# One encoder block on one core: router ahead of the norm, the prompt's sort in pairs of tiles, the two lists and first gathers apart

## The reference, cut to what matters

```python
x = x + concat(yA, yB) @ w_out                      # D = 1024; yA, yB are two attentions
h = rms_norm(x, ffn_norm_w)
aff = softmax(h @ w_router)                          # n tokens x 16 experts
gates, idx = top_k(aff.T, cap)                       # cap = 2 * n / 16: 128 prompt, 32 sample tokens
def expert(idx_e, g_e, wg, wu, wd):                  # D_EXPERT = 2816
    xe = h[idx_e]
    return ((silu(xe @ wg) * (xe @ wu)) @ wd) * g_e
x = x.at[idx].add(experts)
return rms_norm(x, final_norm_w)
```

## Time and profile before

| | us |
|---|---|
| median of 3 runs | 2697.51 (2696.32 to 2697.77) |
| span of the profiled execution, first to last instruction | 2693.8 |
| PE busy | 2606.6 (97%) |
| DVE busy | 1963.9 (73%) |
| ACT busy | 1692.7 (63%) |
| POOL busy | 1108.9 (41%) |

### The profile page before, as it was taken

How to read it: one execution, slowest core, us unless ns; L and a number is a source line. 1 busy time by engine, 2 the same in 40 slices (tenths; PEclk the granted TensorE clock), 3 DMA queues, 4 the chain that set the end, 5 groups by cost and what they waited for, 6 DMA issues and landing times. The chain is left out here.

```text
span 2693.8 us, 53857 instructions
## 1 busy us (share of the span) xinstructions
PE 2606.6 (97%) x22588; PEld 2372.4 (88%) x22588; DVE 1963.9 (73%) x2361; ACT 1692.7 (63%) x2527; POOL 1108.9 (41%) x781
## 2 busy tenths in 40 slices
PE   7999999989959999999999999999999999999997
PEld 6666776665549999999999999999999999999997
DVE  6233256674668788888878888787878878788787
ACT  4366345562127676676767677676766767677675
POOL 2224201134125364452736346263644627354354
PEclk9999999999969999999999999999999999999998
DMA  7311312124557898979889897988988798898887
GB/s 188 76 46 32 74 37 44 36 85 150 168 199 274 314 313 297 330 256 342 293 319 315 292 333 258 340 294 314 322 293 322 269 330 304 311 323 289 317 299 285
DMA packets 365898, 652.18 MB, mean 242 GB/s; under 512 B 26599, under 2 KB 94055, under 8 KB 365623
## 3 DMA queue, kind: packets, MB, share of 16 engines
q1 hardware_dynamic: 349483, 605.63, 64.5%
q0 software_dynamic: 16176, 43.12, 6.3%
HBM read 612.81 MB, written 36.94 MB: 241 GB/s over the span
## 5 line engine op out<-in xcount | busy, mean ns | idle before, releaser
L1986 DVE TENSOR_TENSOR wl<-stg,wh 128x2048 bf16<-128x2048 f32 (+1 forms) x544 | 1241.0, 2289 | 256.6 <-ACT wh L1476 251.8
L1476 ACT ACTIVATE wh<-stg 128x2048 fp32r<-128x2048 f32 (+1 forms) x544 | 1010.9, 1861 | 196.2 <-PE S L1104 71.4
L2379 POOL TENSOR_TENSOR hx<-hh,hx 128x320 fp32r<-128x320 f32 x176 | 385.6, 2191 | 805.9 <-ACT hx L1529 805.6
L1101 PE MATMUL S<-X,wh 128*128 128x320 f32 x3760 | 591.0, 312 | 1.3 <-DVE X L1995 1.3
L1101 PEld LDWEIGHTS S<-X,wh 128*128 128x128 f32 x3760 | 557.1, 189 | 1.7 <-DVE X L1995 1.7
L1147 PE MATMUL S<-hx,wh 128*128 128x320 f32 x1892 | 312.6, 313 | 0.5 <-DVE yTs L2034 0.5
L1101 PE MATMUL OG<-X,wh 128*128 128x320 f32 x1872 | 298.2, 311 | 1.2 <-DVE gg L2016 1.2
L1104 PE MATMUL S<-Xb,wl 128*128 128x160 bf16 x3760 | 290.1, 233 | 0.0
L1147 PEld LDWEIGHTS S<-hx,wh 128*128 128x128 f32 x1892 | 280.8, 188 | 0.9 <-issue 0.6
L1101 PEld LDWEIGHTS OG<-X,wh 128*128 128x128 f32 x1872 | 277.4, 188 | 1.6 <-issue 1.4
L1104 PEld LDWEIGHTS S<-Xb,wl 128*128 128x128 bf16 x3760 | 258.9, 98 | 12.0
(11 more groups left out here) (316 smaller groups left out, 3803.5 us busy)
## 6 DMA issues: line engine op xcount, KB each, us to landing
stg<-in_w_gate_dram SPq DMA_DIRECT2D x80, 2048.0 KB
stg<-in_w_up_dram SPq DMA_DIRECT2D x80, 2048.0 KB
stg<-in_w_down_dram SPq DMA_DIRECT2D x64, 2048.0 KB
stg<-in_w_down_dram SPq DMA_DIRECT2D x32, 1536.0 KB
stg<-in_w_gate_dram SPq DMA_DIRECT2D x16, 1024.0 KB
stg<-in_w_up_dram SPq DMA_DIRECT2D x16, 1024.0 KB
w_st<-in_w_in_dram SPq DMA_DIRECT2D x20, 512.0 KB, 4.0
yt<-mixed SPq DMA_DIRECT2D x10, 512.0 KB, 5.4
```

The costliest lines, as they stand in the source:

```text
L1101: pe.matmul(out, w, x, start=first, stop=False, skip_group_check=True)
L1476: act.activation(piece_conv(wh, g), piece_stage(g), ACT.Copy).then_inc(rounded, 1)
L1986: dve.tensor_tensor(piece_conv(wl, g), piece_stage(g), piece_conv(wh, g).bitcast(F32), ALU.subtract).then_inc(split, 1)
L2379: pool.tensor_tensor(hx[:, f, CT:2 * CT], hh[:, :, :], hx[:, f, 0:CT].bitcast(F32), ALU.subtract).then_inc(hidden_ready, 1)
```

## The change

- **The router goes ahead of the norm.** PE turns `x2t` instead of `h2t`; ACT (not DVE) copies the turned rows to `h2T`. The router matrix is multiplied once by the norm's weight (`fw_cols`, a new load of 1024 single elements; `wrt_scaled`), and each row's 1/rms is applied to the logits (`logits`: one fused multiply and maximum, then a subtraction).
- **Order of a turn.** Turn t now turns tile t-1's sum after two of the eight cross pairs of the first half, and turns its affinities before the last two cross pairs of the second half. Before, the affinities of tile t-2 were turned.
- **The last tile's sum is made in two halves**, as soon as each half is projected.
- **The sort is in pairs of tiles.** `WK` is 112 partitions of 64 values: both tiles of a pair, each in two halves. Eight rounds (the last without a replacement) rank them, `bitonic` steps merge halves, the pair, and the pair with the best so far. `SORTS` spreads these 31 units over turns 2 to 9 and the end. The sample has its own buffer `WS` and its own four rounds at the end.
- **Lists apart.** Cutoff, comparison, ranks and places of the prompt are made before those of the sample; prompt and sample row numbers of the first expert have a matmul and a semaphore step each. POOL gathers 128 prompt rows, then 32 whole sample rows (`xes`, by `idx_first`), in place of the two gathers of quarters. PE turns the prompt rows without waiting for the sample's. Later experts gather as before.

The diff, cut to its core:

```diff
-ROUNDS_AHEAD = {6: (0, 5, 6), 7: (0, 11, 12), 10: (1, 5, 6)}
-ROUNDS_BEHIND = {5: (0, 0, 5), 6: (0, 6, 11), 7: (0, 12, 16), 9: (1, 0, 5), 10: (1, 6, 11), 11: (1, 11, 12)}
+HALF_ROUNDS = 8
+U_PAIR = HALF_ROUNDS + 7
+U_BOTH = U_PAIR + 8
+U_ALL = U_BOTH + 8
+SORT_X2, SORT_H2, SORT_END = range(3)
+SORTS = {(2 * p + 2 + n, at_): (p, u0, u1) for p in range(TPR // 2) for n, at_, u0, u1 in
+         ((0, SORT_END, 0, 2), (1, SORT_X2, 2, 6), (1, SORT_H2, 6, 14), (1, SORT_END, 14, 15),
+          (2, SORT_X2, 15, 21), (2, SORT_H2, 21, U_ALL if p else U_BOTH)) if 2 * p + 2 + n < TT}
...
+                sp.dma_start(fw_cols[:, :], ffn_norm_w[0].rearrange("(k p) -> p k", p=P)).then_inc(wrt_in, 16)
...
-            for t in range(TT + 2):
-                if t < TT:
-                    wo_half(t, 0)
...
-                    pe.wait_ge(h2_ready, t)
-                    for c in range(2):
-                        turn(wo_fill["h", t - 1] + c, [h2t[:, b * P:(b + 1) * P] for b in range(4 * c, 4 * c + 4)])
+            pe.wait_ge(scores_read, 2 * STEPS)
+            for t in range(TT):
                 if t >= 2:
-                    aff_turn(t - 2)
-                if t < TT:
-                    wo_half(t, 1)
-                if 1 <= t <= TT:
-                    router(t - 1)
...
+                    wo_highs(t, 0, range(KT))
+                    wo_crosses(t, 0, (0, 1))
+                    x2_turn(t - 1, 0)
+                    x2_turn(t - 1, 1)
+                    mm = wo_crosses(t, 0, range(2, KT))
+                    if t == TT - 1:
+                        mm.then_inc(mixed_ready, 1)
+                    if t == 1:
+                        pe.wait_ge(wrt_scaled, 1)
+                        pe.wait_ge(out_read, STEPS)
+                    router_parts(t - 1, range(KT))
+                wo_highs(t, 1, range(KT))
+                if t + 1 < TT:
+                    y_turn(t + 1)
+                if t:
+                    router_sum(t - 1)
+                wo_crosses(t, 1, range(KT - 2))
+                if t:
+                    aff_turn(t - 1)
+                wo_crosses(t, 1, (KT - 2, KT - 1)).then_inc(mixed_ready, 1)
+
+            u = TT - 1
+            for c in range(2):
+                x2_turn(u, c)
+                router_parts(u, range(4 * c, 4 * c + 4))
+            router_sum(u)
...
+            index_p(1).then_inc(idx_ps, 1)
+            pe.wait_ge(onehot_ready, 2)
+            index_s(1, bank=1).then_inc(idx_ps, 1)
             pe.wait_ge(gathered, 16)
-            pe.wait_ge(gathered_s, 32)
+            pe.wait_ge(idx_ready, 3)
             for q in range(4):
-                x_turn(q, q)
+                for m in range(2):
+                    d = 2 * q + m
+                    mm = pe.transpose(x_banks[q][:, m * CP:(m + 1) * CP], xe[:, d * P:(d + 1) * P], identf[:, :])
+                mm.then_inc(xturned, 1)
+            pe.wait_ge(gathered_s, 16)
+            for d in range(KT):
+                mm = pe.transpose(S[:, 1, CS * d:CS * d + CS], xes[:, d * P:(d + 1) * P], identf[0:CS, 0:CS])
+            mm.then_inc(xturned, 1)
...
+                    if u < HALF_ROUNDS:
+                        if u == 0:
+                            dve.wait_ge(affT_ready, 2 * p + 2)
+                        eight = ranked[:, 8 * u:8 * u + 8]
+                        own(dve.max(eight, WK[:, :]))
+                        own.wait()
+                        if u < HALF_ROUNDS - 1:
+                            own(dve.match_replace(WK[:, :], eight, WK[:, :], -1.0))
+                            own.wait()
+                    elif u == HALF_ROUNDS:
+                        own(dve.tensor_copy(other[:, 0:64], ranked[64:112, ::-1]))
+                        own.wait()
+                        dve.tensor_tensor(m[0][:, 0:64], ranked[0:48, :], other[:, 0:64], ALU.max)
+                        own(dve.tensor_tensor(m[0][:, 64:128], ranked[0:48, :], other[:, 0:64], ALU.min))
+                        own.wait()
+                    elif u < U_PAIR:
+                        n = u - HALF_ROUNDS
+                        bitonic(m[(n - 1) % 2], m[n % 2], 64 >> n)
...
+                dve.wait_ge(mixed_ready, t)
+                x2_free(u)
+                x2_sum(u, slice(0, D))
+                dve.sem_inc(mixed_read, 1)
+                dve.sem_inc(x2_ready, 1)
+                if (t, SORT_X2) in SORTS:
+                    sort_units(*SORTS[t, SORT_X2])
+                h2_rows(u)
+                if (t, SORT_H2) in SORTS:
+                    sort_units(*SORTS[t, SORT_H2])
+                logits(u)
                 if t + 1 < TT:
                     y_lows(t + 1)
-                if t in ROUNDS_BEHIND:
-                    best_eight(part, 48, min(r0 + 2, r1), r1)
-                if t == 8:
-                    merge(0)
-                if t >= TT:
-                    affT_copy(t - 2)
-
-            dve.wait_ge(affT_ready, TT)
-            best_eight(1, 80, 12, 16)
-            dve.tensor_copy(least[32:48, :], ranked[64:80, 1, P - 1:P].to_broadcast([NE, P]))
-            merge(1)
-            own(dve.tensor_tensor(top2[:, :], merges[:, 2, :], merges[:, 3, ::-1], ALU.max))
+                affinities(u)
+                affT_copy(u)
+                if (t, SORT_END) in SORTS:
+                    sort_units(*SORTS[t, SORT_END])
...
+            x2_sum(u, slice(0, 512))
+            dve.sem_inc(x2_ready, 1)
+            dve.wait_ge(mixed_ready, TT + 1)
+            x2_sum(u, slice(512, D))
+            dve.sem_inc(x2_ready, 1)
+            sort_units(TPR // 2 - 1, U_PAIR, U_BOTH)
+            own(dve.tensor_tensor(best[1][:, :], best[0][:, :], merges[0][0:NE, ::-1], ALU.max))
             own.wait()
-            own(dve.tensor_reduce(cutoff[:, :], top2[:, :], AX_X, ALU.min))
+            own(dve.tensor_reduce(cutoff[:, :], best[1][:, :], AX_X, ALU.min))
             own.wait()
-            dve.tensor_copy(least[0:NE, :], cutoff[:, 0:1].to_broadcast([NE, P])).then_inc(cutoff_ready, 1)
-            dve.wait_ge(cutoff_ps, 1)
-            for t0, t1, e0 in ((0, TPR, 0), (TPR, TT, 32)):
-                lim = S[:, 0, e0:e0 + NE].unsqueeze(1).to_broadcast([P, t1 - t0, NE])
+            dve.tensor_copy(least[0][:, :], cutoff[:, 0:1].to_broadcast([NE, P])).then_inc(cutoff_ready, 1)
+            logits(u)
+            h2_rows(u)
...
+            affinities(u)
+            dve.wait_ge(cutoff_ps, 1)
+            dve.wait_ge(aff_ready, TT)
+            choose(0, TPR, S[:, 0, 256:256 + NE])
+            affT_copy(u)
+            dve.wait_ge(affT_ready, TT)
+            for r in range(CS // 8):
+                eight = ranked_s[:, 8 * r:8 * r + 8]
+                own(dve.max(eight, WS[:, :]))
+                own.wait()
+                if r < CS // 8 - 1:
+                    own(dve.match_replace(WS[:, :], eight, WS[:, :], -1.0))
+                    own.wait()
+            dve.tensor_copy(least[1][:, :], ranked_s[:, CS - 1:CS].to_broadcast([NE, P])).then_inc(cutoff_ready, 1)
...
+            list_places(0, TPR, S[:, 0, 0:2 * TPR * NE].rearrange("p (m t e) -> p m t e", m=2, t=TPR))
+            dve.wait_ge(cutoff_ps, 2)
+            choose(TPR, TT, S[:, 0, 768:768 + NE])
...
+            onehots_p(1).then_inc(onehot_ready, 1)
+            dve.wait_ge(pos_ps, 2)
+            dve.wait_ge(chosen_ready, 2)
+            list_places(TPR, TT, S[:, 0, 512:576].rearrange("p (m t e) -> p m t e", m=2, t=TT - TPR))
+            onehots_s(1).then_inc(onehot_ready, 1)
...
+            pool.wait_ge(h2_stored, 16 * TPR)
+            pool.wait_ge(idx_ready, 1)
+            stand()
+            pool.indirect_dma_start(xe[:, :], None, hn_d,
+                                    bass.IndirectOffsetOnAxis(ap=idx[:, 0, 0:1], axis=0)).then_inc(gathered, 16)
+            pool.wait_ge(h2_stored, 16 * TT)
+            pool.wait_ge(idx_ready, 2)
+            stand()
+            pool.indirect_dma_start(xes[:, :], None, hn_d,
+                                    bass.IndirectOffsetOnAxis(ap=idx_first[:, 0:1], axis=0)).then_inc(gathered_s, 16)
```

494 lines of the change are left out of this document (283 added, 211 removed).

## The result

| | before | after |
|---|---|---|
| median of the runs, us | 2697.51 | 2673.87 (2670.68 to 2675.89, 5 runs) |
| ratio, 95% interval | 1 | 0.9919 (0.9908 to 0.9929) |
| span of the profiled execution | 2693.8 | 2670.6 |
| its own time beside the span | not given | 2672.59 |
| start of the projection to PE's last cross (E) | 135.30 | 133.22 |

The account below looks back on a forecast made before the run. PE's own work bounds the expert stage; before it PE waits in a 42.3 us stretch, mostly for DVE's chain. Gains of 15.9 behind E and 2.1 in the turns, less 0.7, make 17.3 us: 2680.2, range 2676.0 to 2689.

Parts of the forecast that it names:

- So E to experts is 26.4: Behind the projection: from PE's last cross to the first expert matmul 26.4 us for 42.3, a gain of 15.9.
- the expert stage as long as before: From the first expert matmul on: PE's own work, left alone by the change, 1897 us as before.
- the 0.7 for affinities: In the turns: PE's new wait ahead of the last four crosses, 0 to 2.7 us over nine turns, taken as 0.7.
- The slower rival: In the turns: the wait for affinities holds all nine; slower than before from 2.0 us a turn; chance 3%.
- I take 0.55: DVE's sort in the turns: a round on 64 values takes 0.55 us, against 0.97 on 256 values.
- the overflow: In odd turns: short rounds cost as much as long ones, the sort overflows, 2.3 us a turn, 2689; chance 12%.
- 12.0 against 10.1: Odd turns at 0.97 a round: DVE reaches 12.0 us, PE makes logits possible at about 10.1; PE held up 1.7.
- the second half starts at about 1.2: DVE's last-tile sum: affinities' copy, merge step and first half come after E, so the second half starts about 1.2 us.
- a gather that PE waits for more than 4 us behind POOL's start: Sign of being wrong, at the first gather: its data were put at 4.0 us after its start.
- The lower end: Whole kernel: 2676.2 us with the sample's transposes at nothing, affinities never late and no releases; range from 2676.0.
- Two rivals fell: Weights' transfers bound the expert stage, time near 2695, chance 2%; new column load late in turn 1, 2688, chance 1%.
- 1.28 for the copy and the low part: Ahead of the first expert matmul: 1.28 us behind the 16 transposes of 0.235 each, 5.0 together.

Follow-up runs that it names:

- experiment 4: Changed kernel with the affinities' transposes three cross pairs earlier in each of nine turns: 2683.18 us, ratio 0.9956.
- experiment 5: Changed kernel with every MAX8 of the prompt's rounds issued twice, a round of 64 values taking 0.84 us: 2679.77 us, ratio 0.9942.
- the repeat: Changed kernel run again without any edit: 2675.60 us, ratio 0.9931.
- experiment 2: Kernel before with only the first expert's whole-row gathers, prompt rows turned first and the wait for `Xb` moved behind the first high products: ratio 0.9988.
- 11: Kernel before with thirty extra matmuls of 512 columns while PE waits for the first gather: 2692.11 us, ratio 0.9987.
- experiment 6: Changed kernel without the column load of the norm's weight, the router matrix left unscaled: 2674.32 us, ratio 0.9922.
- experiment 3: Changed kernel with PE's wait for `Xb` put back ahead of an expert's first matmul: 2678.75 us, ratio 0.9939.

## Why the prediction was right in kind and 6 us too high

The step that failed is the sum "So E to experts is 26.4": its mechanism and its order of steps are those of the trace, but two terms are too large. The sum of the last tile, put at 2.15 us after E, took 1.4, and the transposes and the split, put at 5.0, took 3.9. With roundings the whole took 24.2. A third term, "the expert stage as long as before", was put at nothing and gave 2.3.

The spans differ by 23.2 us: 0.6 in the start of the projection, which no part of the change explains, 2.1 in the turns, 18.2 from E to the first expert matmul, and 2.3 in the expert stage. The forecast had 0, 1.4, 15.9 and 0. The rest of the 6.3, 0.4 us, lies around the span: it assumed 3.7, and after has 2.0 in its profiled execution and 3.3 from span to median. So of the 6.3 us 2.3 are the chain behind E, 2.3 the expert stage, 0.7 the turns, and 1.0 the start and what lies around the span.

- **In the turns: right.** The wait for `h2t` is gone (2.1). Of the 0.7 for affinities 0.3 came, in one turn of nine. The margin was called 0.25 and is about 0.3 (experiment 4). The slower rival needed 2 us in every turn; even in experiment 4, with the margin taken away, a turn lost 1.0.
- **"I take 0.55" for a round on 64 values: right.** From MAX8 to MAX8 it is 708.37 - 707.79 = 0.58. The Trainium skill, "VectorE: DVE Perf Modes", section on the TRN2 errata, gives the fixed cost of about 150 cycles by which the prediction estimated 0.22 for the MAX8; the trace agrees with 0.23. The same section's advice to tile at 512 elements or more doesn't decide here: the prompt takes 32 rounds in either kernel, and each is 0.39 us shorter. The 12% for the overflow was a fair chance on an open price: at 0.84 it comes true (experiment 5). The prediction's own figures for it, 12.0 against 10.1, give 1.9 and not the 1.7 that it used.
- **The chain behind E: every term on the safe side.** Forecast and measured, in us after E:

| mark | forecast | after |
|---|---|---|
| sum of the last tile done and released | 2.15 | 1.4 |
| cutoff copied | 6.3 | 5.5 |
| prompt compared | 9.0 | 8.1 |
| sample's cutoff copied | 12.9 | 11.9 |
| row numbers | 16.35 | 15.0 |
| POOL's gather starts | 17.35 | 15.9 |
| PE turns the prompt's rows | 21.4 | 20.3 |
| first expert matmul | 26.4 | 24.2 |

  The first term fails already: "the second half starts at about 1.2". It put the copy of the affinities, a merge step and the first half behind E; in the trace copy and step are over before E, at 748.01, since the affinities are turned two cross pairs ahead of it, and both halves take 1.53 from 748.04. That is 0.75 us less. Behind it every stage up to POOL's start came out 0.05 to 0.3 shorter, 0.7 together, by durations and releases rounded up. The gather landed 4.4 us after its start, not 4.0. The prediction named "a gather that PE waits for more than 4 us behind POOL's start" as a sign of being wrong; it came, and the shorter terms hid its 0.4. The last term is the largest: 5.0 us for the transposes and the split took 3.9. The text called 16 equal transposes a bound from above and then used it; the sample's eight, of 32 rows, took 1.06 and not 1.88, and PE waited 0.93 and not 1.28 for the low part behind them.
- **The lower end was no lower end.** It was worked out as 2676.2 from the sample's transposes at nothing and the releases. It left out the chain's first term, the expert stage and the scatter of the run: the forecast started from a median of three runs at 2697.51, and the later sets of runs gave 2696.14, 2695.89 and 2694.69 for the same kernel.
- **"The expert stage as long as before": off by 2.3 us**, and by 1.5 in the repeat. One piece is seen. The waits of PE in the kernel before, from 2600 us on, have a row that after hasn't:

```profile
PE OG L1101 <- DVE gg L2016: 1.2, 1, 1.2
```

  It is in the last expert, where DVE had waited for ACT's rounded weights; the kernel of experiment 2 has it with 0.9, and after with 0.2. ACT in turn had waited for a transfer of weights. Its rows, before and after:

```profile
2611.83 1.91 ACT L1476 ACTIVATE wh<-stg 128x2048 fp32r<-128x2048 f32 x1 [3.90 <-DMA stg<-in_w_up_dram]
...
2589.26 1.91 ACT L1563 ACTIVATE wh<-stg 128x2048 fp32r<-128x2048 f32 x1 [2.93 <-DMA stg<-in_w_up_dram]
```

  The repeat has 2.69 there, and experiments 2 and 11, on the kernel before, 3.61 and 3.39. So some 1.6 us of the 2.3 lie in the last expert. Another 0.6 come from the clock in the first 32 products (6.9 us before, 6.3 after from the first to the 33rd): it rose 3.3 us after the first expert matmul in after and 4.7 before. In the repeat it rose 4.8 after it, and this part is gone. In between the two traces keep step within 0.3 us. Why the last expert's weights land about 1 us less late stays open.
- **Two rivals fell, one with a remainder.** The weights didn't become the bound of the stage: it kept its pace at an earlier start. ACT waits four times in it for a transfer, 6.3 us together before and 5.1 after, the longest in the last expert. The load is hidden (experiment 6).
- **One thing was right by luck.** "1.28 for the copy and the low part" silently assumed that `Xb` isn't waited for. With the wait where it stood, this step would have missed by 4.5 us the other way (experiment 3). The diff showed the moved wait and the earlier trace rows the gathers around it; the prediction didn't ask what the four casts now stand behind.

What the gain of 18.2 us behind E is made of, as far as runs separate it: 2.9 the gathers and the first expert's start, with the moved wait in it; 1.0 the prompt's gather ahead of the sample's numbers, which experiment 2 doesn't have; 0.8 the sum in halves; the rest, some 13.5, the sort in the turns with the router ahead of the norm, and the other parts of the lists. These last were not run one by one, and how they share it isn't shown; the rows above place it, with the cutoff 17.0 us sooner after E.

## What to carry to other kernels

Where one engine runs a serial chain while the main engine waits, list that chain instruction by instruction from rows and add it up without padding; ask of each bound that you use as a value whether the piece is really as large as the one measured. When a transfer is regrouped, follow every reader of its buffer, not only the first: here four casts moved behind the last piece, and 4.5 us hung on one wait. Work that moves off the chain may cost more in sum and still pay: DVE's 12 us more in the turns cost PE 0.3 us of waiting. And when the main engine idles ahead of its main stage, look at the granted clock behind the wait: matmuls without a reader are worth some 3 us at either length of the wait.
